# A decoder layer on one core: the part behind the experts, with the order of its products changed

## The chip, the cores and the metric

The kernel runs on one core of one Trainium2 chip. A core has TensorE (PE: matrix products, results in PSUM), VectorE (DVE), ScalarE (ACT), GpSimd (POOL) and SyncE (SP, which here only issues DMAs). Each engine works through its own list of instructions in order, and engines wait for one another by semaphores. PSUM has eight banks of 128 x 512 f32. The metric is the device time of one launch in microseconds (us); lower is better.

## The reference, cut to what matters

One layer for 1024 prompt positions and 8 x 4 sample positions. Up to the experts, nothing is changed. Behind them, what is computed is

```python
h = h + hierarchical_moe(...)                          # 16 experts, each token uses two
e = rms_norm(p_i @ w_ple, norm_ple)                    # (rows, 256) @ (256, 1024)
gate = jax.nn.sigmoid(rms_norm(h, norm_pg) @ w_pg)     # (rows, 1024) @ (1024, 1024)
h = h + gate * e
y = rms_norm(h, norm_final)
```

The rows are 1056, so there are nine tiles of up to 128 rows; the last one has 32.

## The kernel before

**Products.** A product in f32 is made from three products in a reduced format: each operand is split into a high part (rounded by ScalarE) and a low part (the rest, by VectorE), and `product3` (L711 to L719) issues for each 128 of the contraction high x high (L716), low weight x high (L717) and high weight x low (L718). A tile's embedding product (`c_ple`) is 12 matmuls of 512 columns, its gate product (`c_gate`, two halves) is 48. `transposes` (L463) turn 128 x 128 blocks through PSUM: 8 for a tile's normalised rows (`c_rows`), 2 for its embedding input (`c_embed`).

**Experts.** A block is 128 gathered rows through one expert. Weights of expert e+1 are split in pieces A0, A1, B, D0, D1 (ScalarE L1471, L1476; VectorE L1187, L1177) while expert e runs. After a block its result is copied to `yb` and stored to `y_rows` (L1521). For the part behind the experts, `w_pg` takes the place of an expert's gate and up weights (A0, A1, B) and `w_ple` that of its down weights (D0). In the last block, B and D0 are split only after the block's result has been copied out.

**The part behind the experts** works tile by tile on one set of buffers. Its first tiles and last tiles are written out, those between are loops (`Fori`).

- SP waits until the last block has been stored, then raises `blocks_over` (L433 to L435), and loads the embedding input of a tile (`p_load`, L424) and stores the output of the tile before (L429).
- POOL, `c_gather` (L1731 to L1740): the two expert results of each row are fetched by two indirect DMAs into `ya` and `y2`, after the indices have been copied to `index_u` (L1737). The gather of tile t+2 waits for `c_head` of tile t+1. POOL also computes the factors of the three norms (`rstd`: L1634, L1636, L1638) and the normalised rows `an` (L1747).
- DVE, `c_head` (L1262, L1264): h += gate weight x gathered row, twice. `c_en` (L1282, L1285) scales the embedding product, `c_blend` (L1293, L1295) forms h + gate x e, `c_out` (L1302) writes the output row; `c_anT` and `c_pT` make the low parts (L1177).
- ACT: sums of squares of h (`c_hsq`, L1565), of the embedding product (`c_esq`, L1570, L1571) and of the final h (`c_fsq`, L1581), the sigmoid (L1576), and the high parts (`c_pT` L1551, `c_anT` L1557, L1559).
- PE: for each tile gate half 0, embedding transposes of the next tile, gate half 1, row transposes of the next tile, embedding product of the next tile. ACT starts the stage with `c_hsq(0)`, and so does DVE with `c_head(0)`; the first embedding product waits behind both.

## Time and profile before

| | |
|---|---|
| runs (3) | 1328.31, 1332.95, 1333.29 us; median 1332.95 |
| profiled execution, its own time (span, first to last instruction) | 1329.0 us |
| mean granted clock of TensorE, of 2.4 GHz | 0.962 |
| busy: PE, DVE, ACT, POOL | 1211.2 (91%), 701.7 (53%), 505.0 (38%), 213.2 us (16%) |
| last matmul of the last block, first product of the stage | 1141.8 us, 1158.4 us |
| last product of the stage, end | 1318.3 us, 1329.0 us |

The trace is one execution. Times in the rows are from the start of the span. `1.00` as granted clock is 2.4 GHz, the lower level is 1.2 GHz. A bracket behind a row is the idle time of that engine before it and what ended it. Durations of matmuls overlap, so that the distance between two starts is the cost of one.

### The profile page before, as it was taken

The numbers are of one execution on the slowest core, as the hardware profiler recorded it, in microseconds if no ns is written. First come the engines' busy times: TensorE is split into PE (matmuls) and PEld (weight loads), VectorE is DVE, ScalarE is ACT, GpSimd is POOL, SyncE is SP. The second block draws the span as 40 slices with busy tenths as digits, with TensorE's granted clock in tenths as the row PEclk, the third lists the DMA queues.
The fourth block names the chain that finished last, engine by engine and source line by source line (L and its number), as shares of the span: only waits on it lengthen the run. The fifth ranks groups of instructions, "written<-read, shape, count | busy, mean of one in ns | idle before, by whom it ended". The sixth has DMA issues, their size and how long they took to land.

```text
span 1329.0 us, 17507 instructions
## 1 busy us (share of the span) xinstructions
PE 1211.2 (91%) x6065; PEld 860.7 (65%) x6066; DVE 701.7 (53%) x1343; ACT 505.0 (38%) x860; POOL 213.2 (16%) x336
## 2 busy tenths in 40 slices
PE   2999999999999999989659999999999999599886
PEld 1454555565655554435259899988989999477663
DVE  1344343434343434333665986599966662545454
ACT  0222222213131313121325875588855551433332
POOL 3320202020202020010100000000000000254452
PEclk9999999999999999998669999999999999799998
DMA  9700000000000000024394995599996564223320
GB/s 317 288 1 1 16 0 16 0 16 0 16 0 16 0 17 0 19 73 151 122 289 169 374 369 209 215 373 369 376 368 219 203 212 159 68 68 103 103 76 36
DMA packets 122092, 180.28 MB, mean 136 GB/s; under 512 B 7795, under 2 KB 96479, under 8 KB 122066
## 3 DMA queue, kind: packets, MB, share of 16 engines
q1 hardware_dynamic: 108078, 144.60, 31.9%
q0 software_dynamic: 6512, 21.77, 4.8%
q10 hardware_dynamic: 7476, 13.57, 2.7%
q8 instruction: 15, 0.25, 0.1%
q14 instruction: 11, 0.09, 0.0%
HBM read 151.96 MB, written 27.96 MB: 135 GB/s over the span
## 4 chain that ended last, share of the span: by engine, by line
PE 71%; DMA 7%; DVE 7%; ACT 5%; POOL 5%; issue 3%; ACTq 2%; SPq 0%; POOLq 0%; DVEq 0%
PE bank L457 36%; PE bank L716 10%; PE bank L718 9%; PE bank L717 9%; PE bank L463 4%; DMA raw_gu<-in_w_up 3%; DMA rows<-y_rows,index_u 3%; PE bank L629 1%; DVE w_lo L1187 1%; POOL work_c L1747 1%; POOL small L1636 1%; POOL small L1634 1%; ACT w_hi L1471 1%; DVE work L982 1%; ACT L1415 1%
## 5 line engine op out<-in xcount | busy, mean ns | idle before, releaser
L457 PE MATMUL bank<-weights,work 128*128 128x512 f32 (+3 forms) x1152 | 456.0, 553 | 1.9 <-DVE work L851 1.5
L457 PEld LDWEIGHTS bank<-weights,work 128*128 128x128 f32 (+1 forms) x1152 | 196.2, 182 | 242.4 <-issue 241.7
L716 PE MATMUL bank<-w_hi,xh 128*128 128x256 f32 x768 | 220.3, 287 | 2.7 <-DVE xl L1177 2.7
L718 PE MATMUL bank<-w_hi,xl 128*128 128x256 f32 x768 | 218.2, 284 | 0.0
L717 PE MATMUL bank<-w_lo,xh 128*128 128x256 f32 x768 | 218.2, 284 | 0.0
L1187 DVE SCALAR_TENSOR_TENSOR w_lo<-raw_gu,cols,w_hi 128x512 fp32r<-128x512 f32 x272 | 183.2, 746 | 8.9 <-ACT w_hi L1471 8.2
L1471 ACT ACTIVATE w_hi<-raw_gu,cols 128x512 fp32r<-128x512 f32 x272 | 170.5, 714 | 32.4 <-PE bank L718 19.0
L716 PEld LDWEIGHTS bank<-w_hi,xh 128*128 128x128 f32 x768 | 147.9, 193 | 4.2 <-issue 3.1
L717 PEld LDWEIGHTS bank<-w_lo,xh 128*128 128x128 f32 x768 | 148.1, 193 | 0.8
L718 PEld LDWEIGHTS bank<-w_hi,xl 128*128 128x128 f32 x768 | 147.9, 193 | 0.0
L1634 POOL TENSOR_TENSOR small<-small,norm_c 128x1 f32<-128x1 f32 (+1 forms) x54 | 24.2, 448 | 531.9 <-ACT work L1411 297.2
L716 PE MATMUL bank<-w_hi,hid_hi 128*128 128x512 f32 x192 | 78.5, 409 | 0.0
L1177 DVE TENSOR_TENSOR w_lo<-raw_d,w_hi 128x1024 fp32r<-128x1024 f32 x66 | 77.5, 1216 | 0.1
L885 DVE COPY work<-bank 128x512 f32<-128x512 f32 (+1 forms) x9 | 6.2, 690 | 132.8 <-PE bank L457 132.8
L717 PE MATMUL bank<-w_lo,hid_hi 128*128 128x512 f32 x192 | 75.0, 391 | 0.0
L718 PE MATMUL bank<-w_hi,hid_lo 128*128 128x512 f32 x192 | 75.0, 390 | 0.0
L1720 POOL COPY index_u<-token_u 128x1 uint32 (+1 forms) x25 | 4.9, 198 | 427.6 <-PE bank L463 405.8
L851 DVE TENSOR_TENSOR work<-bank,cols 128x512 f32<-128x512 f32 (+1 forms) x27 | 16.5, 640 | 99.1 <-PE bank L463 99.1
L1476 ACT ACTIVATE w_hi<-raw_d 128x1024 fp32r<-128x1024 f32 x66 | 66.0, 1050 | 7.0 <-DVE yb L1232 4.0
L716 PE MATMUL bank<-w_hi,a_hi 128*128 128x512 f32 (+1 forms) x144 | 58.3, 405 | 2.7 <-DVE a_lo L1177 2.7
L1386 ACT ACTIVATE work<-bank 128x512 f32<-128x512 f32 (+1 forms) x9 | 5.4, 596 | 142.4 <-PE bank L457 142.4
L717 PE MATMUL bank<-w_lo,a_hi 128*128 128x512 f32 (+1 forms) x144 | 56.8, 395 | 0.0
(285 smaller groups left out, 1660.6 us busy)
## 6 DMA issues: line engine op xcount, KB each, us to landing
raw_gu<-in_w_gate SPq DMA_DIRECT2D x32, 1024.0 KB, 7.5
raw_gu<-in_w_up SPq DMA_DIRECT2D x32, 1024.0 KB, 10.2
raw_d<-in_w_down SPq DMA_DIRECT2D x16, 2048.0 KB, 12.4
y_rows<-yb ACTq DMA_DIRECT2D x24, 512.0 KB, 6.3
weights<-in_w_in SPq DMA_DIRECT2D x3, 2048.0 KB, 15.6
weights<-in_w_in SPq DMA_DIRECT2D x1, 4096.0 KB, 21.7
weights<-in_w_out SPq DMA_DIRECT2D x1, 4096.0 KB, 25.4
m_rows<-work SPq DMA_DIRECT2D x8, 512.0 KB, 2.6
```

The source lines that it names most:

```text
L457: last = nc.tensor.matmul(out, lhs(k), rhs(k), start=(k == ks[0]), stop=(k == ks[-1]))
L463: last = nc.tensor.transpose(out[:, (c - lo) * P:(c - lo) * P + T], src[0:T, c * P:c * P + w], ident[0:T, 0:T])
L629: last = nc.tensor.matmul(bank[4][0:T, hh * HP:(hh + 1) * HP], dec[0:T, hh, 0:T], xdt[0:T, hh * HP:(hh + 1) * HP], start=True, stop=True)
L716: nc.tensor.matmul(out, lh(k), rh(k), start=(k == 0), stop=False)
L717: nc.tensor.matmul(out, lh(k), rl(k), start=False, stop=False)
L718: last = nc.tensor.matmul(out, ll(k), rh(k), start=False, stop=(k == (K or len(ks)) - 1))
L851: return V.tensor_tensor(dst[:, :, 0:T], src_bank.rearrange("p (c t) -> p c t", c=4)[:, :, 0:T], bc(cols[:, c0:c0 + 4], P, 4, T), ALU.mult)
L1177: return V.tensor_tensor(out, x, hi.bitcast(F32), ALU.subtract)
L1187: ins = V.scalar_tensor_tensor(out=gu_lo[:, k, :, cols_], in0=raw_gu[q // KC][:, k, :, :], scalar=gain(e, k), in1=gu_hi[:, k, :, cols_].bi ...
L1471: ins = A.activation(gu_hi[:, k, :, cols_], raw_gu[q // KC][:, k, :, :], ACT.Copy, scale=gain(e, k))
L1476: ins = A.activation(d_hi[:, ks, :], raw_d[:, ks, :], ACT.Copy)
L1634: own.did(G.tensor_tensor(var[0:T], sum_[0:T], norm_eps[count][0:T, :], ALU.add))
```

## The change

- The stage is in two phases. First all nine embedding products, then all gate products. Everything is unrolled.
- The embedding products use three pairs of PSUM banks in turn (0/1, 4/5, 6/7), the gate products two pairs (0/1, 4/5), and transposed embedding inputs and transposed rows have banks 2 and 3. PSUM is declared as one tensor, so that one instruction can read two banks: the square, the scaling and the low and high parts of a tile are one instruction each where there were two.
- `e` is kept for all nine tiles (`en[t]`), and the output row is written over it. `ya`, `y2`, `p_in`, `p_hi`, `p_lo`, `a_hi`, `a_lo` exist twice; each tile has its own norm factors. The sigmoid is written in place in PSUM.
- `w_ple` is split inside the last block, into a place of its own (`wp_hi`, `wp_lo`), before the block's result is copied out. The second half of `w_pg` (B) is split during the first embedding products (`pg_hi`, `pg_lo`).
- Gathers of tiles 0 to 3 and the heads of tiles 0 and 1 fall into the first phase. Indices go to the indirect DMA without a copy. `c_blend` works on halves.
- Ahead of the stage only semaphores are merged under fewer names; the order of what waits for what is the same.

```diff
+        en = [placed(f"en{t}", (B0 + 4 * GU + 4 * D * t) if t < DC else (B0 + 4 * (GU + DN) + 4 * GU + 4 * D * (t - DC)) if t < 2 * DC else C1, D)[:, :]
+              for t in range(TILES)]
...
+            for t in range(2, TILES):
+                sp.wait_ge(s("pTp_done"), t - 1)
+                p_load(t)
+            sp.wait_ge(s("w_split"), PG_SPLIT)
+            sp.dma_start(fin_row, i["norm_final"].partition_broadcast(P)).then_inc(s("fin_row_loaded"), 16)
+            for t in range(TILES):
+                out_store(t)
...
+            def c_ple(t):
+                T = rows(t)
+                pe.wait_ge(s("pT_ready"), t + 1)
+                if t == 2:
+                    pe.wait_ge(s("bank6_free"), total1)
+                    pe.wait_ge(s("bank7_free"), total1)
+                if t >= 3:
+                    pe.wait_ge(s("en_ready"), t - 2)
...
+            def c_gate(t, half):
+                T = rows(t)
+                pe.wait_ge(s("anT_ready"), t + 1)
+                if t < 2:
+                    pe.wait_ge(s("en_ready"), TILES - 2 + t)
+                else:
+                    pe.wait_ge(s("blend_done"), 2 * t - 3 + half)
...
+            pe.wait_ge(s("w_split"), PLE_SPLIT)
+            for t in range(TILES):
+                c_ple(t)
+                if t + 2 < TILES:
+                    c_embed(t + 2)
+                if t == TILES - 2:
+                    c_rows(0)
+            pe.wait_ge(s("w_split"), PG_SPLIT)
+            for t in range(TILES):
+                c_gate(t, 0)
+                if t + 1 < TILES:
+                    c_rows(t + 1)
+                c_gate(t, 1)
...
                     split(e + 1, "A1")
+                    for k in range(PC):
+                        dve.wait_ge(s("w_high"), PG_A + k + 1)
+                        lo(wp_lo[:, k, :], raw_d[:, k, :], wp_hi[:, k, :]).then_inc(s("w_split"), 1)
                 dve.wait_ge(s("down_done"), n)
...
+            def c_head(t):
+                T = rows(t)
+                dve.wait_ge(s(f"ya{t % 2}_loaded"), 16 * (t // 2 + 1))
+                own.did(V.scalar_tensor_tensor(out=hrow(t), in0=ya[t % 2][0:T, :], scalar=gates[0:T, 0, t:t + 1], in1=hrow(t), op0=ALU.mult, op1=ALU.add))
+                dve.wait_ge(s(f"y2{t % 2}_loaded"), 16 * (t // 2 + 1))
+                own.wait()
+                V.scalar_tensor_tensor(out=hrow(t), in0=y2[t % 2][0:T, :], scalar=gates[0:T, 1, t:t + 1], in1=hrow(t), op0=ALU.mult, op1=ALU.add
+                                       ).then_inc(s("hc_ready"), 1)
...
+            def c_en(t):
+                T = rows(t)
+                dve.wait_ge(s("re_ready"), t + 1)
+                V.scalar_tensor_tensor(out=en[t][0:T, :], in0=pair((0, 4, 6)[t % 3])[0:T, :], scalar=re_[t][0:T, :], in1=ple_row[0:T, :],
...
+            def c_blend(t, half):
+                T = rows(t)
+                part = slice(half * BANK, (half + 1) * BANK)
+                dve.wait_ge(s("sig_ready"), 2 * t + half + 1)
+                if half == 0:
+                    dve.wait_ge(s("en_ready"), t + 1)
+                V.tensor_tensor(en[t][0:T, part], bank[(0, 4)[t % 2] + half][0:T, :], en[t][0:T, part], ALU.mult).then_inc(s("blend_done"), 1)
+                dve.wait_ge(s("blend_done"), 2 * t + half + 1)
+                V.tensor_tensor(hhalf(t, half), hhalf(t, half), en[t][0:T, part], ALU.add).then_inc(s("hf_ready"), 1)
...
+            c_pT(0)
+            c_pT(1)
+            pg_lo(range(0, 2))
+            dve.wait_ge(s("ple_row_loaded"), 16)
+            for t in range(TILES):
+                c_en(t)
+                if t + 2 < TILES:
+                    c_pT(t + 2)
+                if t < 3:
+                    pg_lo(range(2 * t + 2, 2 * t + 4))
+                if t == 2:
+                    c_head(0)
+                if t == 5:
+                    c_head(1)
+            c_anT(0)
+            dve.wait_ge(s("fin_row_loaded"), 16)
+            for t in range(TILES):
+                if t:
+                    c_blend(t - 1, 1)
+                if t + 2 < TILES:
+                    c_head(t + 2)
+                if t:
+                    c_out(t - 1)
+                c_blend(t, 0)
+                if t + 1 < TILES:
+                    c_anT(t + 1)
+            c_blend(TILES - 1, 1)
+            c_out(TILES - 1)
...
                     split(e + 1, "A1")
+                    act.wait_ge(s("d_loaded"), 16 * (NE + 1))
+                    act.wait_ge(s("w_split"), PG_A)
+                    for k in range(PC):
+                        A.activation(wp_hi[:, k, :], raw_d[:, k, :], ACT.Copy).then_inc(s("w_high"), 1)
                 act.wait_ge(s("down_done"), n)
...
                 act.dma_start(y_rows[bass.ds(b * P, P), :], yb).then_inc(s("y_stored"), 16)
-                if not more:
-                    split(e + 1, "B")
-                    split(e + 1, "D0")
...
+            def pg_hi(ks):
+                for k in ks:
+                    if k == 0:
+                        act.wait_ge(s("gu1_loaded"), 32 * (NE + 1))
+                    A.activation(gu_hi[:, k, :, HE:], raw_gu[1][:, k, :, :], ACT.Copy, scale=gain(NE, k)).then_inc(s("w_high"), 1)
...
+            def c_esq(t):
+                T = rows(t)
+                act.wait_ge(s("ple_done"), t + 1)
+                if t == TILES - 1:
+                    act.wait_ge(s("w_split"), PG_SPLIT)
+                A.activation(en[t][0:T, :], pair((0, 4, 6)[t % 3])[0:T, :], ACT.Square, accum_out=sse[t][0:T, :]).then_inc(s("sse_ready"), 1)
...
+            for t in range(TILES):
+                c_esq(t)
+                if t + 2 < TILES:
+                    c_pT(t + 2)
+                if t < 3:
+                    pg_hi(range(2 * t + 2, 2 * t + 4))
+                if t == 4:
+                    c_hsq(0)
+                if t == 6:
+                    c_hsq(1)
+            c_anT(0)
+            for t in range(TILES):
+                if t:
+                    c_sig(t - 1, 1)
+                if t + 2 < TILES:
+                    c_hsq(t + 2)
+                if t:
+                    c_fsq(t - 1)
+                c_sig(t, 0)
+                if t + 1 < TILES:
+                    c_anT(t + 1)
+            c_sig(TILES - 1, 1)
+            c_fsq(TILES - 1)
...
+            def c_gather(t):
+                T = rows(t)
+                if t >= 2:
+                    pool.wait_ge(s("hc_ready"), t - 1)
+                for q, dst, name in ((0, ya, "ya"), (1, y2, "y2")):
+                    pool.indirect_dma_start(dst[t % 2][0:T, :], None, y_rows[0:BLOCKS * P, :],
+                                            bass.IndirectOffsetOnAxis(ap=slots_u[0:T, q, t:t + 1], axis=0)).then_inc(s(f"{name}{t % 2}_loaded"), 16)
...
+            c_gather(0)
+            c_re(0)
+            c_re(1)
+            c_gather(1)
+            for t in range(2, 5):
+                c_re(t)
+            c_an(0)
+            c_gather(2)
+            for t in range(5, TILES):
+                c_re(t)
+            c_gather(3)
+            c_an(1)
+            for t in range(TILES):
+                if t:
+                    c_rf(t - 1)
+                if t + 2 < TILES:
+                    c_an(t + 2)
+                if t + 4 < TILES:
+                    c_gather(t + 4)
+            c_rf(TILES - 1)
```

## Rows read from the trace of the kernel before

**Rows 1.** The page: TensorE's busy tenths in 40 slices of the span

```profile
PE   2999999999999999989659999999999999599886
```

**Rows 2.** Busy times by stretch; columns: us, PE, PEld, DVE, ACT, POOL, PEclk, DMA

```profile
1224.10:1242.70 18.60, 16.74 (x79) 13.41 (x78) 9.15 (x11) 6.12 (x13) 9.12 (x15) 1.00 0.26 92
```

**Rows 3.** Chain that ended last, at the stage's begin; columns: start, us, what

```profile
1142.86 2.62 DMA y_rows<-yb
...
1146.40 1.19 POOL rows L1739
...
1148.39 5.24 DMA rows<-y_rows,index_u
...
1156.42 1.15 ACT work_c L1565 x2
1157.57 0.28 ACT p_hi L1551
1157.87 0.44 DVE p_lo L1177
```

**Rows 4.** The same chain, through one tile of the loop

```profile
1205.42 1.16 ACT work_c L1565 x2
...
1209.01 1.90 POOL work_c L1747
...
1214.86 6.17 DMA rows<-y_rows,index_u
1221.29 1.30 DVE h L1262
...
1224.14 1.16 ACT work_c L1565 x2
```

**Rows 5.** TensorE in order of time, one tile; start, us, line, operation, count

```profile
1180.23 1.04 PE L463 MATMUL bank<-ident,work_c 128*128 128x128 f32 x8
1181.02 0.47 PE L716 MATMUL bank<-w_hi,p_hi 128*128 128x512 f32 x1
...
1183.90 0.50 PE L716 MATMUL bank<-w_hi,a_hi 128*128 128x512 f32 x1
...
1195.18 1.03 PE L463 MATMUL bank<-ident,work_c 128*128 128x128 f32 x8
```

**Rows 6.** TensorE in order of time, after idle times (in brackets)

```profile
1158.44 0.77 PE L716 MATMUL bank<-w_hi,p_hi 128*128 128x512 f32 x1 [16.42 <-DVE p_lo L1177]
...
1163.70 1.10 PE L463 MATMUL bank<-ident,work_c 128*128 128x128 f32 x8
...
1248.28 1.09 PE L463 MATMUL bank<-ident,work_c 128*128 128x128 f32 x8 [1.59 <-POOL work_c L1747]
1251.13 0.50 PE L716 MATMUL bank<-w_hi,p_hi 128*128 128x512 f32 x1 [1.76 <-DVE p_lo L1177]
...
1255.23 0.63 PE L716 MATMUL bank<-w_hi,a_hi 128*128 128x512 f32 x1
```

**Rows 7.** VectorE and ScalarE in order of time, around the experts' end

```profile
1138.64 2.73 DVE L1187 SCALAR_TENSOR_TENSOR w_lo<-raw_gu,cols,w_hi 128x512 fp32r<-128x512 f32 x4
...
1148.17 1.99 ACT L1476 ACTIVATE w_hi<-raw_d 128x1024 fp32r<-128x1024 f32 x2
...
1149.32 2.35 DVE L1177 TENSOR_TENSOR w_lo<-raw_d,w_hi 128x1024 fp32r<-128x1024 f32 x2
```

**Rows 8.** VectorE in order of time, in the first tile

```profile
1166.09 1.29 DVE L1177 TENSOR_TENSOR a_lo<-bank,a_hi 128x512 fp32r<-128x512 f32 x2 [7.80 <-ACT a_hi L1559]
...
1170.96 0.75 DVE L1282 SCALAR_TENSOR_TENSOR work_c<-bank,small,ple_row 128x512 f32<-128x512 f32 x1
```

**Rows 9.** The chain that ended last, its end

```profile
1318.35 0.59 ACT work_c L1576
...
1321.52 1.05 ACT work_c L1581
...
1323.90 1.27 DVE rows L1302
```

436 lines of the change are left out of this document (157 added, 279 removed).

## The prediction

> **What bounds the kernel now.** I read the page first, for where TensorE is less than full: it is busy in nine tenths of nearly every slice, and the dip near the end is where the changed stage begins [rows 1]. Everything ahead of the last block is untouched, so the question is the 187.2 us from the last block's last matmul (1141.8) to the end (1329.0). Second, the chain that ended last, at the stage's begin: result stored, indices copied, gathers issued, rows landed at 1153.6, the head of h, its square, and only then the first embedding input is split [rows 3], so that TensorE stands still for 16.42 us, although the embedding product needs nothing of h [rows 6]. Third, the same chain inside the loop: it runs through square, norm, gather, a transfer of 6.17 us and the head, from 1205.42 to 1224.14, 18.7 us for a tile [rows 4], and TensorE comes into it nowhere. TensorE's own work for a tile is 15.0 us (1180.23 to 1195.18, without idle time) [rows 5]; in a loop tile it is busy for 16.74 of 18.6 us [rows 2] and pays short waits, of which some pull its clock down. So the stage is bound by a chain through one pair of gather buffers, some 3.7 us a tile above TensorE.
>
> **Prices.** From starts in [rows 5], at 2.4 GHz: 8 row transposes 0.8, embedding product 2.9, two gate halves with 2 embedding transposes between 11.3 (a half 5.6). At 1.2 GHz an embedding product takes 5.26 (1158.44 to 1163.70) [rows 6]. A square of 1024 columns takes 1.2 [rows 4]; a square and the norm factor behind it 2.4 (1321.52 to 1323.90) [rows 9]; a low part of 1024 columns 1.3, of 256 columns 0.4 [rows 3, 8]; a head 2 x 1.3 [rows 4]; scaling by `c_en` is two halves of 0.75 now and one instruction afterwards, 1.3 to 1.5, I take 1.3 since a head instruction of that width takes that [rows 4, 8]; a pair of gathers is two issues of 1.2 [rows 3]. The sigmoid that writes PSUM has no row. Its nearest is the one that writes SBUF, 0.6 [rows 9]; I take 0.6 and give it 0.5 to 0.8.
>
> **Step 1, the start.** In the last block VectorE ends piece A1 at 1141.37 [rows 7]. Behind it now come two copies for `wp_hi` on ScalarE (1.0 each, to 1143.4) and two low parts on VectorE (1.18 each, to 1144.9) [rows 7]. Queued behind these are the copies of the result to `yb`: VectorE's half ends at 1145.6, so the store, issued at 1142.86 now, and `blocks_over` come 2.8 us later. Who waits for that is the gathers, and they no longer stand before TensorE. ScalarE, which issues the store, goes on at 1146.2; high and low part of the first embedding input (0.3 and 0.4 [rows 3]) give the first product at 1147.1 instead of 1158.4: **11.3 us gained**. TensorE idles 5 us there, not 16.4.
>
> **Step 2, nine embedding products.** TensorE would need 9 x 2.9 + 7 x 0.15 + 0.8 = 28 us. But it is not what bounds them. The input of tile t+2 is split by VectorE behind `c_en(t)`, hence: end of product t, square and norm 2.4, `c_en` 1.3, low part 0.4, and some 0.3 of signalling, 4.4 us until product t+2 may start. Two tiles then take 4.4 + 2.9 = 7.3 us, 3.7 a tile. Twice it is worse. `c_head(0)` (2.6) and pieces of `w_pg` (1.4) are queued on VectorE ahead of `c_en(3)`: product 5 is about 2 us late. On POOL the normalised rows of tile 0 (factor 1.2, rows 1.90 [rows 4]) and the gather of tile 2 (2.4) are queued ahead of the norm factor of tile 5: product 7 is some 1.2 us late. `c_head(1)` then holds VectorE ahead of `c_en(6)`, and with it the input of product 8, by about 1 us. Laid out instruction by instruction, with product 0 at 5.1 (low clock after 5 us idle), this gives the products' starts 1147.1, 1152.4, 1156.7, 1160.4, 1164.0, 1169.7, 1172.7, 1178.1, 1182.3 and the last end at 1185.2. Then a seam: the first gate product waits for square and norm of tile 8 (2.4), `c_en(8)` 1.3 and the low part of the rows of tile 0, 1.3, together 5.2 with signalling: 1190.4. I add 2 us for product starts at the low clock after the idle times of 2 to 3 us, part of it hidden, and 1 us for POOL, whose small operations are slower beside VectorE: **first gate product at 1193.5**.
>
> **Step 3, nine gate products.** TensorE: 18 x 5.57 + 8 x 0.8 = 106.7. The chain here, from the end of gate half 1 of a tile: sigmoid 0.6, blend of half 1 1.4, head of a later tile 2.7, its square 1.2, final square and norm 2.4, output row 1.3, blend of half 0 1.4, low part 1.3, signalling 0.4: 12.7 us until the gate product after next may start. TensorE is free for it after 11.95 (one tile). The rest, 0.75, is paid every second tile, or 0.4 a tile: 3.2 in all. One more low-clock piece behind the 5 us seam: in the loop before, 1.59 and 1.76 us of idle time close together were followed by an embedding product of 4.1 us (1251.13 to 1255.23) instead of 2.9 [rows 6]; I take 1.6. Last gate product ends at 1193.5 + 106.7 + 3.2 + 1.6 = **1305.0**, against 1318.3.
>
> Gathers stand on nothing here: the gather of tile t+4 is issued in tile t, and 6.2 us of transfer [rows 4] lie beside two tiles of 12. If that cover were gone, each tile would pay up to 6 us.
>
> **Step 4, the end.** 10.7 us from the last matmul to the end now. The blend works on the half that is left, two operations of 0.65 instead of two of 1.22: 1.1 less. End 1305.0 + 9.6 = 1314.6.
>
> **The sum.** 1329.0 - 1314.6 = 14.4 us in the profiled execution, whose span lies 4 us under the median of the runs. Taken from the median: 1332.95 - 14.4 = **1319**. Its own range is 1312 to 1326 (`c_en` and sigmoid at either end, signalling, clock). The seam of unrolled code has no price in the trace: the two unrolled last tiles of before show no idle time other than that for data, so I put it at 0 to 2 us.
>
> **Rivals.** (a) The clock stays at 2.4 GHz: a loop tile in which TensorE did nothing for 1.9 of 18.6 us has a granted clock of 1.00 [rows 2], and the new idle times are mostly 0.7 us a tile. Then the 2 and 1.6 fall away, and most of the slow first product is hidden anyway by the chain; POOL isn't slowed (1 us): -19.0, 1314. 18%.
> (b) The opposite: TensorE is at 80% in the embedding phase, with an idle time in every tile, and stays at 1.2 GHz there. Nine products of 5.26 with their transposes are 50 us, now themselves the bound, and the first gate product starts at 1203.8; the time is 1329, no change that can be told. For it: 1.59 + 1.76 us of idle time were enough once [rows 6]. 12%.
> The Trainium skill, "TensorE: Matmul & The Clock Gate", section "A second HAM failure mode: psum-queue depth-cycling", speaks for (b): products that cycle through PSUM banks with micro-idle times between them make the clock swing. By it the sum would be that of (b) or a little under; by the single rows above it is mine.
> (c) The chain of step 3 is longer, for instance because POOL's norm factor meets a busy VectorE (from the square's end at 1206.58 to 1209.01 it took 2.4 us in the loop [rows 4], against 1.2 at the end) and VectorE's order makes everybody wait. At 14.7 us instead of 12.7 each tile costs 1 us more, 7 to 8 us in all: 1326. 10%.
> (d) Slower than before: as (b), and the low clock lasts into the gate products, since now they wait in every second tile. A 512-column matmul costs 0.2 us more there [rows 6], so beyond (b) it takes 54 of them, little more than one tile, to be 0.5% slower; at two tiles 1348. Against it: gate tiles keep TensorE 97% busy. 6%.
> My forecast 54%.
>
> **Numbers.** 0.5% (6.7 us) is about what a measurement of this kernel can tell from no change; the runs of before spread by 5 us. Faster: forecast, (a) and half of (c), 77%; same: (b) and the rest of (c), 17%; slower: 6%. The range reaches from (a) with its own 4 us to (b): 1309 to 1330.
>
> **What would show it.** In the profile of the changed kernel: the first embedding product 5 us behind the last block's last matmul (step 1); starts of embedding products 3.5 to 4 us apart, with TensorE waiting for the low part of the embedding input (step 2); 5 us of idle time before the first gate product; gate tiles 12.3 us apart, with no wait for gathered rows anywhere (step 3); 9.6 us at the end (step 4). It is wrong if the granted clock is low through the first phase, if gate tiles are over 13 us apart, or if a gather or a load of embedding input ends a wait.

## The result and the profile after

| | before | after |
|---|---|---|
| median of the runs | 1331.01 us (4 runs, 1328.31 to 1333.29) | 1311.30 us (4 runs, 1310.36 to 1311.70) |
| ratio, 95% interval | | 0.9852 [0.9832, 0.9872] |
| profiled execution, span | 1329.0 | 1309.2 |
| mean granted clock | 0.962 | 0.967 |
| last block's end to first product | 16.8 | 5.6 |
| first product to end of the last | 159.9 | 153.5 |
| end of the last product to the end | 10.7 | 9.5 |

The change makes the kernel 1.5% faster, some 20 us where 14.4 were predicted. Of the 19.8 us between the two spans, 1.0 lies ahead of the stage, where the work is the same. The rest is 11.2 at the start, 6.4 between the products and 1.2 at the end.

Since the time ahead of the stage differed by up to 2.6 us from trace to trace with the same work in it, I compare below the *stage*: from TensorE's transposes of the first embedding inputs (right behind the last block's last matmul, at 1141.64 before and 1140.64 after) to the end. It is 187.4 us before and 168.6 after.

The page after, TensorE and its granted clock in 40 slices. It answers to [rows 1], where slice 35 is at 5 tenths and slices 38 and 39 at 8. Now slices 35 to 37, the embedding phase and the seam behind it, are at 7 to 8 tenths, 38 and 39 are full, and the clock's last dip lies in slice 37. The dips around slice 20 lie ahead of the stage in both.

```profile
PE   2999999999999999998749999999999999878997
...
PEclk9999999999999999997759999999999999998999
```

Busy times by stretch: the wait at the start, the embedding phase, the seam, the gate phase, the end. Columns as in [rows 2]: us, PE, PEld, DVE, ACT, POOL, granted clock, DMA share, GB/s.

```profile
1140.60:1146.20 5.60, 0.64 (x5) 0.37 (x4) 3.52 (x5) 3.32 (x6) 0.00 (x0) 0.74 0.11 45
1146.20:1185.20 39.00, 32.15 (x130) 23.90 (x130) 22.66 (x28) 17.43 (x35) 19.13 (x34) 0.91 0.38 123
1185.20:1190.10 4.90, 0.03 (x1) 0.02 (x1) 2.59 (x4) 2.01 (x3) 3.01 (x5) 0.75 0.11 13
1190.10:1299.70 109.60, 108.53 (x496) 84.56 (x496) 60.15 (x64) 34.90 (x56) 51.70 (x67) 0.98 0.26 89
1299.70:1309.20 9.50, 0.00 (x0) 0.00 (x0) 2.63 (x3) 1.71 (x3) 0.95 (x3) 0.71 0.06 14
```

TensorE is full in the gate phase (108.53 of 109.60) and in no other stretch. In the embedding phase it does nothing for 7 of 39 us. (The seam is the idle time between the last embedding product and the first gate product.)

TensorE after, in order of time; brackets as in [rows 6]. These are the transposes at the stage's begin, products 0, 2, 5 and 7 (counted from 0), the row transposes of tile 0, the first gate half, the row transposes behind it, and one of the later gate products that had to wait.

```profile
1140.64 0.60 PE L467 MATMUL psum<-ident,p_in 128*128 128x128 f32 x4
...
1146.22 0.77 PE L720 MATMUL psum<-wp_hi,p_hi 128*128 128x512 f32 x1 [4.98 <-DVE p_lo L1174]
...
1155.18 0.50 PE L720 MATMUL psum<-wp_hi,p_hi 128*128 128x512 f32 x1 [0.99 <-DVE p_lo L1174]
...
1168.31 0.50 PE L720 MATMUL psum<-wp_hi,p_hi 128*128 128x512 f32 x1 [2.17 <-DVE p_lo L1174]
...
1176.98 0.51 PE L720 MATMUL psum<-wp_hi,p_hi 128*128 128x512 f32 x1 [2.44 <-DVE p_lo L1174]
...
1181.43 1.04 PE L467 MATMUL psum<-ident,an 128*128 128x128 f32 x8
...
1190.11 0.76 PE L720 MATMUL psum<-w_hi,a_hi 128*128 128x512 f32 x1 [4.88 <-issue]
...
1197.68 1.03 PE L467 MATMUL psum<-ident,an 128*128 128x128 f32 x8
...
1216.33 0.50 PE L720 MATMUL psum<-w_hi,a_hi 128*128 128x512 f32 x1 [0.37 <-DVE a_lo L1174]
```

Every wait of the embedding phase ends with the low part of an embedding input (products 2, 3, 4, 5 and 7 wait, for 0.99, 0.48, 0.74, 2.17 and 2.44 us; 1, 6 and 8 do not). The first product stands behind 4.98 us of idle time instead of 16.42 [rows 6]. The first gate half takes 7.6 us (1190.11 to 1197.68) where one takes 5.6 at full clock [rows 5].

The chain that ended last, after, through one gate tile; start, us, what. It answers to [rows 4].

```profile
1204.21 0.59 ACT psum L1586
...
1204.83 0.70 DVE en L1292
...
1206.24 1.21 DVE h L1263
...
1208.86 1.16 ACT dump L1574 x2
...
1210.10 1.16 ACT dump L1594 x2
...
1211.60 0.58 POOL small L1646
...
1213.73 0.69 DVE en L1292
...
1214.44 0.69 DVE h L1294
...
1215.14 1.14 DVE a_lo L1174
...
1216.33 0.50 PE psum L720
```

The gathers have gone from the chain; the sigmoid, both halves of the blend, a head, two squares and the norm are what is left. From 1204.18, the end of a product, to 1216.33 this takes 12.15 us. TensorE's own work between these two points takes 11.78, and the rest, 0.37, is the idle time in the row of 1216.33 above. Such a wait occurs three times in the whole phase.

### The profile page after: what moved, and what is told of

Read it like the earlier page. It is cut to its first block, busy times and chain, and to the rows that moved or that the text cites. A ratio compares the mean times of both kernels' runs of the same rounds, so it can differ in the third digit from the quotient of the medians.

```text
span 1309.2 us, 17273 instructions
## 1 busy us (share of the span) xinstructions
PE 1208.6 (92%) x6065; PEld 859.7 (66%) x6066; DVE 702.2 (54%) x1343; ACT 501.1 (38%) x833; POOL 203.6 (16%) x309
## 4 chain that ended last, share of the span: by engine, by line
PE 75%; DVE 9%; ACT 4%; issue 4%; DMA 3%; POOL 2%; ACTq 2%; DVEq 0%; SPq 0%; POOLq 0%; another core or an unknown queue 0%
PE psum L461 36%; PE psum L720 11%; PE psum L722 10%; PE psum L721 10%; PE psum L467 5%; DVE w_lo L1184 2%; DMA raw_gu<-in_w_up 1%; PE psum L633 1%; DVE work L979 1%; ACT L1410 1%; ACTq L1344 1%; PE psum L639 1%; DMA weights<-in_state_ssm 1%; DMA xg<-m_rows,index_u 1%; PE psum L616 0%
## 5 line engine op out<-in xcount | busy, mean ns | idle before, releaser
L461 PE MATMUL psum<-weights,work 128*128 128x512 f32 (+3 forms) x1152 | 455.7, 552 | 1.9 <-DVE work L848 1.5
L461 PEld LDWEIGHTS psum<-weights,work 128*128 128x128 f32 (+1 forms) x1152 | 196.2, 182 | 242.1 <-issue 241.4
L720 PE MATMUL psum<-w_hi,xh 128*128 128x256 f32 x768 | 220.3, 287 | 2.7 <-DVE xl L1174 2.7
L722 PE MATMUL psum<-w_hi,xl 128*128 128x256 f32 x768 | 218.2, 284 | 0.0
L721 PE MATMUL psum<-w_lo,xh 128*128 128x256 f32 x768 | 218.2, 284 | 0.0
L720 PEld LDWEIGHTS psum<-w_hi,xh 128*128 128x128 f32 x768 | 147.8, 193 | 4.2 <-issue 3.1
L721 PEld LDWEIGHTS psum<-w_lo,xh 128*128 128x128 f32 x768 | 148.0, 193 | 0.8
L722 PEld LDWEIGHTS psum<-w_hi,xl 128*128 128x128 f32 x768 | 147.8, 192 | 0.0
L1644 POOL TENSOR_TENSOR small<-small,norm_c 128x1 f32<-128x1 f32 (+1 forms) x54 | 17.2, 319 | 553.3 <-ACT work L1406 297.2
L720 PE MATMUL psum<-w_hi,hid_hi 128*128 128x512 f32 x192 | 78.6, 409 | 0.1
L722 PE MATMUL psum<-w_hi,hid_lo 128*128 128x512 f32 x192 | 75.1, 391 | 0.0
## 6 DMA issues: line engine op xcount, KB each, us to landing
raw_d<-in_w_down SPq DMA_DIRECT2D x16, 2048.0 KB, 12.1
```

What stands on the lines that cost most here:

```text
L461: last = nc.tensor.matmul(out, lhs(k), rhs(k), start=(k == ks[0]), stop=(k == ks[-1]))
L720: nc.tensor.matmul(out, lh(k), rh(k), start=(k == 0), stop=False)
L721: nc.tensor.matmul(out, lh(k), rl(k), start=False, stop=False)
L722: last = nc.tensor.matmul(out, ll(k), rh(k), start=False, stop=(k == (K or len(ks)) - 1))
L1644: own.did(G.tensor_tensor(var[0:T], sum_[0:T], norm_eps[count][0:T, :], ALU.add))
```

## The experiments

Stage lengths and starts are from one trace each, ratios from the medians of 3 to 5 rounds. "Start" is from the stage's begin to the first embedding product, "middle" from there to the last product's end.

| kernel | stage | start | middle | ratio to before [95%] |
|---|---|---|---|---|
| before | 187.4 | 16.8 | 159.9 | |
| after | 168.6 | 5.6 | 153.5 | 0.9852 [0.9832, 0.9872] |
| e1_unroll | 182.8 | 16.6 | 155.4 | 0.9954 [0.9940, 0.9969] |
| e2_gather_first | 179.0 | 17.2 | 151.1 | 0.9941 [0.9924, 0.9958] |
| e9_old_order | 172.3 | 16.8 | 144.7 | 0.9901 [0.9886, 0.9917] |
| e3_head_first | 178.7 | 14.9 | 154.3 | 0.9929 [0.9912, 0.9946] |
| e4_one_set | 168.4 | 5.5 | 153.3 | 0.9859 [0.9842, 0.9875] |
| e5_split_late | 168.6 | 5.6 | 153.4 | 0.9869 [0.9852, 0.9886] |
| e12_kept_busy | 164.9 | 5.6 | 149.8 | 0.9840 [0.9827, 0.9853] |
| e6_pT_first | 166.1 | 5.6 | 151.0 | 0.9829 [0.9816, 0.9843] |
| e7_seam | 166.1 | 5.6 | 150.9 | 0.9846 [0.9833, 0.9860] |
| e8_both | 163.6 | 5.6 | 148.5 | 0.9816 [0.9803, 0.9830] |
| e10_tuned | 160.9 | 5.6 | 145.8 | 0.9822 [0.9809, 0.9835] |
| e11_tuned_early | 160.7 | 3.7 | 147.4 | 0.9823 [0.9804, 0.9843] |

### One part of the change alone, in the kernel before

**e1_unroll** writes out the five loops of the stage and leaves everything else.

```diff
-            with pe.Fori(1, NT - 1) as t:
-                c_tile(t, pe.snap(t + 1))
+            for t in range(1, NT - 1):
+                c_tile(t, t + 1)
```

> The kernel before with the five loops of the last stage written out and nothing else changed. In its loop, instructions that wait for a register's value show 0.15 to 0.4 us of idle time each (head to head, norm factor to rows, copy of the index to gather), some 1.0 to 1.3 us in the chain of one tile; six tiles are in the loops. My theory: 6 to 8 us faster, 0.995 of before. Rival (the gain is in the order and the buffers, unrolling gives nothing): 1.000. Rival (unrolling is most of it): 0.985.

The stage is 4.6 us shorter, less than the 6 to 8 expected. The chain that ended last, one tile of e1_unroll, start, us, what: squares of h in two tiles that follow one another.

```profile
1203.21 1.16 ACT work_c L1565 x2
...
1221.08 1.16 ACT work_c L1565 x2
```

A tile is 17.9 us instead of 18.7 [rows 4], through the same operations. Of the 0.85 us, some 0.55 are short idle times of the kind that the expectation names (norm factor to rows, index copy to gather, landed rows to head, head to head: 0.1 to 0.2 us less each), and 0.25 is the transfer behind the second gather, 5.92 us instead of 6.17. The prediction had spoken only of the seams of unrolled code, at 0 to 2 us; that loops cost something, it had not priced.

**e2_gather_first** keeps the loops and moves GpSimd's gather of tile t+2 ahead of the normalised rows and of the final norm factor.

```diff
                 c_re(t, n)
+                if not (isinstance(t, int) and t >= NT - 1):
+                    c_gather(t + 2, None, n2)
                 if rows(t) != S:
                     c_an(t + 1, n2)
                 if p is not None:
                     c_rf(t - 1, p)
-                if not (isinstance(t, int) and t >= NT - 1):
-                    c_gather(t + 2, None, n2)
```

> The kernel before, loops and single buffers kept; only on POOL the gather of tile t+2 is placed ahead of the normalised rows of tile t+1 and the final norm factor. Head 2.7, two index copies and issues 2.5 to 3, transfer 5 to 6, head: 11 to 12 us, shorter than TensorE's 15.0. My theory (the loop was bound by POOL's order, which put norm and rows into the gathers' chain): tiles come every 15 to 16 us instead of 18.7, 14 to 20 us faster, 0.987. Rival (one set of gather buffers is what binds): 18 us a tile still, 0.998 to 1.000.

The expectation was too high: the stage is 8.4 us shorter, a tile 16.9 us. Of e2_gather_first: GpSimd's normalised rows, VectorE's output row, and embedding products of two tiles in TensorE's list, each in order of time.

```profile
1208.27 1.89 POOL L1747 TENSOR_TENSOR work_c<-h,small 128x1024 f32<-128x1024 f32 x1 [0.19 <-POOL small L1638]
...
1211.39 1.28 DVE L1302 SCALAR_TENSOR_TENSOR rows<-h,small,rows 128x1024 f32<-128x1024 f32 x1 [6.09 <-POOL small L1638]
...
1213.06 0.50 PE L716 MATMUL bank<-w_hi,p_hi 128*128 128x512 f32 x1 [0.34 <-DVE p_lo L1177]
...
1229.95 0.53 PE L716 MATMUL bank<-w_hi,p_hi 128*128 128x512 f32 x1 [1.75 <-DVE p_lo L1177]
```

The gather has left the chain, as it should, and a second queue stands behind it. GpSimd computes the final norm factor only after the normalised rows (till 1210.16), VectorE stands idle for 6.09 us before its output row that needs the factor, and the low part of the next embedding input is queued on VectorE behind the output row. So TensorE waits for something that never needed the factor.

**e9_old_order** takes e1 and e2 together and also moves VectorE's output row behind the low parts.

```diff
                 c_en(t, n)
-                if p is not None:
-                    c_out(t - 1, p, ...)
                 if more:
...
                     c_anT(t + 1, n2)
+                if p is not None:
+                    c_out(t - 1, p, ...)
```

> The kernel before with one set of buffers, tile by tile as it was, in three orders only: loops written out; on POOL the gather of tile t+2 ahead of the normalised rows of tile t+1; on VectorE the low parts for tile t+1 ahead of the output row of tile t-1, which in the run with the gather first had become what TensorE waited for. Theory (the loop's loss was the order on the helping engines, not the tile-by-tile plan): tiles 15.0 to 15.8 us apart instead of 18.7, last product 18 to 22 us earlier, start of the stage as before: 14 to 19 us faster than before, 0.987. Rival (tile by tile can't be brought near TensorE's 15 us): over 16.5 us a tile, 0.992 or above.

The stage is 15.1 us shorter with one set of buffers, one tile at a time; between the medians it is 12.7 us, less than the 14 to 19 expected. TensorE in e9_old_order, row transposes of tiles that follow one another:

```profile
1210.29 1.09 PE L463 MATMUL bank<-ident,work_c 128*128 128x128 f32 x8 [0.89 <-POOL work_c L1747]
...
1226.33 1.10 PE L463 MATMUL bank<-ident,work_c 128*128 128x128 f32 x8 [0.86 <-POOL work_c L1747]
```

A tile is 16.04 us, of which TensorE's work is 15.0 [rows 5] and 0.86 is this wait. The middle is 144.7 us, **8.8 us shorter than that of the changed kernel**. So the two phases are not what makes the middle shorter: the order in the lists of GpSimd and VectorE does it, and the embedding phase, where TensorE idles, gives a part of that back. What the changed kernel has over e9_old_order is the start: 11.2 us, and for that it does need the phases. In e9_old_order GpSimd ends the normalised rows of tile 0, which need gathered rows, at 1161.92, and TensorE turns them at 1163.78, right behind the first embedding product. Had that product come earlier, the gate product behind it could have come at most 1.9 us earlier. The changed kernel fills that time with further embedding products.

### One part of the change undone

**e3_head_first** puts the head of tile 0 ahead of the first embedding input on VectorE, as it stood before.

```diff
+            c_head(0)
             c_pT(0)
...
-                if t == 2:
-                    c_head(0)
```

> The changed kernel with VectorE's head of tile 0 moved back ahead of the first embedding input, as before the change. Theory: the first embedding product starts 16 to 17 us behind the last block's last matmul instead of 5.6; product 5 no longer waits for that head (2 us back); the kernel is 8 to 10 us slower than the changed one, 0.992 of before. Rival (the early start is lost again in waits behind it, since the gathers and norms come no earlier): 0 to 2 us slower than the changed one, 0.986.

TensorE in e3_head_first, the first embedding product:

```profile
1156.03 0.77 PE L720 MATMUL psum<-wp_hi,p_hi 128*128 128x512 f32 x1 [14.27 <-DVE p_lo L1174]
```

The start is 14.9 us instead of the 16 to 17 expected, the stage 10.1 longer. Products 4 and 5 start 3.7 us apart, 5.4 in the changed kernel, where that head stands between them: the 1.7 us come back, as expected. A single place in VectorE's list carries most of what the start gained, since in it stands the wait for a store and two gathers.

**e4_one_set** uses one pair of gather buffers (`ya[0]`, `y2[0]`) for all tiles and puts the gather of tile t+3 first in GpSimd's tile.

```diff
-                if t >= 2:
-                    pool.wait_ge(s("hc_ready"), t - 1)
+                if t >= 1:
+                    pool.wait_ge(s("hc_ready"), t)
...
-                    pool.indirect_dma_start(dst[t % 2][0:T, :], ...
+                    pool.indirect_dma_start(dst[0][0:T, :], ...
...
             for t in range(TILES):
+                if t + 3 < TILES:
+                    c_gather(t + 3)
                 if t:
...
-                if t + 4 < TILES:
-                    c_gather(t + 4)
```

> The changed kernel with one set of ya and y2 instead of two: a gather waits for the head of the tile before, and stands on POOL right behind that head's turn. Theory (two sets aren't needed when POOL's order is right; head 2.7 + issue 2.4 + transfer 5 is 10 to 11 of 12 us): gate tiles stay 12.0 to 12.5 us apart, 0 to 2 us slower than the changed one, 0.985 to 0.987 of before. Rival (the second set is what took the gathers out of the chain): gate tiles 14 us or more apart, 10 us or more slower, 0.993 or above.

Stage and median stay as they were. GpSimd in e4_one_set, first gathers of two tiles:

```profile
1219.96 1.06 POOL L1747 DMA_INDIRECT ya<-y_rows,slots_u  x1 [3.88 <-DVE h L1266]
...
1232.53 1.06 POOL L1747 DMA_INDIRECT ya<-y_rows,slots_u  x1 [4.67 <-DVE h L1266]
```

GpSimd idles until a head has freed the buffers, for 3.9 to 4.7 us in the later tiles (2.78 and 7.15 at the first two), and the rows have a tile of 12 us to come. Only the head of tile 2, at the seam, waits for its rows (2.45 us), and TensorE does not wait for it. Once the gather stands first in GpSimd's tile, the second pair of gather buffers buys nothing. One pair with the gather in its old place wasn't tried in this plan.

**e5_split_late** splits `w_ple` behind the copies of the last block's result instead of ahead of them.

```diff
-                    for k in range(PC):
-                        dve.wait_ge(s("w_high"), PG_A + k + 1)
-                        lo(wp_lo[:, k, :], raw_d[:, k, :], wp_hi[:, k, :]).then_inc(s("w_split"), 1)
                 dve.wait_ge(s("down_done"), n)
...
                 V.tensor_copy(yb[:, BANK:], bank[7][:, :]).then_inc(s("bank7_free"), 1)
+                if not more:
+                    for k in range(PC):
+                        ...
```

> The changed kernel with the split of w_ple moved back behind the copy of the last block's result, on ScalarE and VectorE. Theory (the early start comes from the embedding products no longer standing behind the head, not from where w_ple is split): result stored 2 to 3 us earlier, w_ple split 2 to 3 us later but next to the same copies, first embedding product 5.5 to 6 us behind the last block's last matmul as in the changed kernel; 0 to 1 us, 0.985 of before. Rival (the split inside the block bought part of the start): the first product 2 to 3 us later, 0.987.

No change: 168.6 us, first product after 5.60 instead of 5.58, although the result's store is issued 2.9 us earlier, counted from the stage's begin. The four pieces have to be done before the first product on either side of the copies.

### What the low clock costs

**e12_kept_busy** adds 18 matmuls of 512 columns, whose results nobody uses, in each of the two 5 us stretches in which TensorE had nothing to do.

```diff
             pe.wait_ge(s("xT_ready"), total1)
+            for _ in range(18):
+                nc.tensor.matmul(bank[0][:, :], hid_hi[:, 0, :], ...
             pe.wait_ge(s("w_split"), PLE_SPLIT)
...
             pe.wait_ge(s("w_split"), PG_SPLIT)
+            pe.wait_ge(s("en_ready"), TILES - 2)
+            for _ in range(18):
+                nc.tensor.matmul(bank[0][:, :], wp_hi[:, 0, 0:P], ...
```

> The changed kernel with 18 matmuls of 512 columns that nothing uses in each of TensorE's two idle times of 5 us (before the first embedding and before the first gate product). It adds work and should only keep the clock up. Theory: first embedding product 2.9 instead of 4.8 us, first gate half 5.7 instead of 7.7, 3 to 4 us faster than the changed kernel, 0.982 to 0.983. Rival (what follows waits for other chains, so that the clock costs nothing at the first place): 2 us, 0.984. Rival (the clock falls all the same): 0 to 1 us slower, 0.986.

TensorE in e12_kept_busy, in order of time: the unused matmuls at the start, product 0, the first gate half behind the unused matmuls of the seam.

```profile
1141.11 4.35 PE L810 MATMUL psum<-hid_hi 128*128 128x512 f32 x18
...
1146.34 0.47 PE L720 MATMUL psum<-wp_hi,p_hi 128*128 128x512 f32 x1 [0.88 <-DVE p_lo L1179]
...
1188.44 0.50 PE L720 MATMUL psum<-w_hi,a_hi 128*128 128x512 f32 x1 [0.74 <-DVE a_lo L1179]
```

Busy times by stretch in e12_kept_busy, the embedding phase with the seam, and the gate phase; columns as above.

```profile
1146.30:1188.40 42.10, 34.82 (x148) 25.78 (x148) 25.27 (x31) 19.36 (x38) 23.12 (x39) 0.96 0.34 115
1188.40:1296.10 107.70, 106.64 (x496) 83.07 (x496) 60.25 (x64) 34.90 (x56) 51.81 (x67) 1.00 0.26 90
```

The chains are as they were (only the transposes of tile 2 now wait 0.33 us for their load), and TensorE starts each phase at full clock: product 0 takes 3.0 us instead of 4.8 (to the end of its last matmul), and the granted clock of the gate phase is 1.00 instead of 0.98. From the stage's begin the first gate product comes after 47.7 us instead of 49.5, and the last one ends after 155.4 instead of 159.0. So work in these two idle times gives back 1.8 us ahead of the gate phase and 1.9 in it, 3.7 in all. That is not the whole cost of the low clock: product 7, behind 0.87 us, is now at full clock, but product 5, behind 2.20 us, fell to the low one (4.38 us from its start to the transposes behind it), which it did not behind 2.17 us in the changed kernel (2.86). The medians' interval does not tell this kernel from the changed one; the trace does.

### Better orders within the new plan

**e6_pT_first** puts the split of the embedding input of tile t+2 ahead of the square and the scaling of tile t, on both engines (ScalarE has the same exchange with `c_esq`).

```diff
             for t in range(TILES):
-                c_en(t)
                 if t + 2 < TILES:
                     c_pT(t + 2)
+                c_en(t)
```

> The changed kernel; in the embedding phase ScalarE and VectorE split the embedding input of tile t+2 ahead of the square and the scaling of tile t instead of behind them. Theory (these products wait for a chain through square, norm and scaling that they don't need): products 3.0 to 3.3 us apart, first product to the end of the ninth 30 to 34 us instead of 39, 5 to 8 us faster than the changed kernel, 0.980 of before. Rival (VectorE or the norms are the limit anyway, since the third pair of banks comes free only behind the scaling): starts stay 3.6 us or more apart, 0.985.

TensorE in e6_pT_first, product 5:

```profile
1167.74 0.50 PE L720 MATMUL psum<-wp_hi,p_hi 128*128 128x512 f32 x1 [3.29 <-DVE p_lo L1174]
```

The theory holds up to product 4: products 2 to 4 start 3.0 to 3.4 us apart from the one before instead of 3.7 to 4.2. Then product 5 waits 3.29 us, because its input is now queued directly behind the head of tile 0, and it runs at the low clock. What was expected to fall to 30 to 34 us, first product to end of the ninth, is 36.7. The stage is 2.5 us shorter where 5 to 8 were expected.

**e7_seam** splits the normalised rows of tile 0 before the square and the scaling of tile 8.

```diff
             for t in range(TILES):
+                if t == TILES - 1:
+                    c_anT(0)
                 c_en(t)
...
-            c_anT(0)
```

> The changed kernel; the rows of tile 0 are split ahead of the square and scaling of tile 8. Theory: the 4.9 us of idle time between the last embedding product and the first gate product go down to 1 us or less, and with them the piece at 1.2 GHz behind it (first gate half 5.7 instead of 7.7 us): 5 to 6 us faster than the changed kernel, 0.981 of before. Rival (the clock falls there whatever the idle time): 3 to 4 us, 0.983.

TensorE in e7_seam, the first gate half and the row transposes behind it:

```profile
1187.59 0.47 PE L720 MATMUL psum<-w_hi,a_hi 128*128 128x512 f32 x1 [0.44 <-issue]
...
1196.43 1.09 PE L467 MATMUL psum<-ident,an 128*128 128x128 f32 x8 [3.12 <-POOL an L1759]
```

The seam has closed, from 4.88 us to 0.44, and the first gate half runs at full clock (5.7 us). But then TensorE waits 3.12 us for the normalised rows of tile 1, which GpSimd computes behind the norm factor of tile 8 and the gather of tile 3. That gives half of it back: the stage is 2.5 us shorter where 5 to 6 were expected.

**e8_both** has both edits.

> Both orders of the two kernels above together. Theory: the gains add, 10 to 13 us faster than the changed kernel, 0.976 of before. Rival (the first is only a shift of waits to the seam or the heads): no more than the better of the two alone, 0.980 to 0.981.

163.6 us, 5.0 shorter: the sum of the two, not the more that was expected, though for another reason than I thought. Product 5 still waits for 3.29 us. The wait of 3.12 us for the rows of tile 1 has gone, but in its place the seam is 1.86 us and the first gate half takes 7.3 us again, at the low clock.

**e10_tuned** takes e8 and moves the waits' causes: the heads of tiles 0 and 1 are split in two, one instruction each in tiles 2 and 3, 5 and 6; the square of h of tile 1 comes a tile later; GpSimd computes the normalised rows of tile 1 ahead of the norm factor of tile 8.

```diff
-                if t == 2:
-                    c_head(0)
-                if t == 5:
-                    c_head(1)
+                if t in (2, 3):
+                    c_head(0, t - 2)
+                if t in (5, 6):
+                    c_head(1, t - 5)
...
             for t in range(5, TILES):
+                if t == TILES - 1:
+                    c_an(1)
                 c_re(t)
             c_gather(3)
-            c_an(1)
```

> The kernel with both orders (0.9816), and: the normalised rows of tile 1 on POOL ahead of the norm factor of tile 8 and the gather of tile 3 behind it; the heads of tiles 0 and 1 in two instructions in two different embedding tiles instead of one; the square of the head of tile 1 one tile later. Theory (in that kernel a head stands ahead of the split of an input, 3.3 us of idle time and a product at 1.2 GHz behind it, and the seam waits for the heads too): 3 to 5 us faster than it, 0.978 to 0.979. Rival (VectorE, busy for 26 of about 30 us in the embedding phase, is the limit): 0 to 1.5 us, 0.981.

The trace's stage is 2.7 us shorter than that of e8_both where 3 to 5 were expected, and the medians' intervals cover one another. In this trace the first gate half is at full clock behind a seam of 1.86 us, as long as that of e8_both, which makes 1.8 of the 2.7 us; that the new order gave them isn't shown. Product 5 still waits 1.94 us and TensorE now waits 2.40 us before the row transposes of tile 0, until VectorE has read the last embedding input from the bank that they write.

**e11_tuned_early** takes e10 and splits the first two embedding inputs in the last block, ahead of the copies of its result.

```diff
+                    for k in range(2):
+                        dve.wait_ge(s("ph_ready"), k + 1)
+                        lo(p_lo[k][:, :, :], bank[2 + k]...).then_inc(s("pT_ready"), 1)
                 dve.wait_ge(s("down_done"), n)
...
-            c_pT(0)
-            c_pT(1)
```

> The one above, and the first two embedding inputs are split inside the last block, ahead of the copies of its result. Theory: first embedding product 3.6 to 3.9 us behind the last block's last matmul instead of 5.6; gathers 0.8 us later, which nobody waits for; 1.5 to 2.5 us faster than the one above. Rival (the later gathers come back as a wait of head 0): no gain.

TensorE in e11_tuned_early, behind product 0:

```profile
1150.67 0.44 PE L467 MATMUL psum<-ident,p_in 128*128 128x128 f32 x2 [1.36 <-DMA p_in<-in_p_prompt]
```

The first product comes after 3.7 us as expected, but the stage is only 0.2 us shorter instead of 1.5 to 2.5. The transposes of tile 2 now wait for its load, which SyncE issues behind its wait for the stored result, and with them product 1, which starts 9.85 us after the stage's begin instead of 10.08. Together e8, e10 and e11 are the fastest kernels here, at 0.982 of before, and the runs do not order them.

## Why the prediction was right, and where it was off

The time fell by more than predicted but within the range, 1311.3 against 1319 in 1309 to 1330. Of the 7.3 us between my unrounded sum (1318.55) and the median, 1.9 are the distance of a profiled span from its median, 4.0 before and 2.1 after. (Against the median of the four runs in the table, 1331.01, it is 2.0 before: the 4.0 came from a median of three runs and is nothing of the kernel.) 1.0 is the time ahead of the stage. The rest, 4.4, is in the terms of the sum.

**Step 1, the start: held.** 5.58 us from the stage's begin to the first product, 5.5 predicted. e3_head_first shows the cause by putting it back. One detail of it was idle: whether `w_ple` is split before or after the copies makes no difference (e5_split_late).

**Step 2, the embedding products: the layout held, the additions did not.** Starts from the stage's begin, in us:

| product | 0 | 1 | 2 | 3 | 4 | 5 | 6 | 7 | 8 | end |
|---|---|---|---|---|---|---|---|---|---|---|
| predicted | 5.5 | 10.8 | 15.1 | 18.8 | 22.4 | 28.1 | 31.1 | 36.5 | 40.7 | 43.6 |
| measured | 5.6 | 10.3 | 14.5 | 18.3 | 22.2 | 27.7 | 30.7 | 36.3 | 41.6 | 44.6 |

Both causes of late products are in the trace. VectorE after, in order of time: the head of tile 0 (its first instruction), `c_en(3)`, the low part for product 5, and `c_en(5)`.

```profile
1164.07 1.28 DVE L1263 SCALAR_TENSOR_TENSOR h<-ya,gates,h 128x1024 f32<-128x1024 f32 x1
...
1166.65 1.28 DVE L1278 SCALAR_TENSOR_TENSOR en<-psum,small,ple_row 128x1024 f32<-128x1024 f32 x1
1167.85 0.41 DVE L1174 TENSOR_TENSOR p_lo<-psum,p_hi 128x256 fp32r<-128x256 f32 x1
...
1175.31 1.28 DVE L1278 SCALAR_TENSOR_TENSOR en<-psum,small,ple_row 128x1024 f32<-128x1024 f32 x1 [5.36 <-POOL small L1648]
```

GpSimd after, in order of time: normalised rows of tile 0, the gather of tile 2 (its first issue), the norm factor of tile 5 (its first operation).

```profile
1169.70 1.90 POOL L1757 TENSOR_TENSOR an<-h,small 128x1024 f32<-128x1024 f32 x1
1171.76 1.07 POOL L1747 DMA_INDIRECT ya<-y_rows,slots_u  x1 [0.17 <-issue]
...
1174.10 0.21 POOL L1644 TENSOR_TENSOR small<-small,norm_c 128x1 f32<-128x1 f32 x1
```

`c_en(3)` starts only when the head ends, and product 5 behind it at 1168.31; the norm factor that `c_en(5)` needs (5.36 us of idle time before it) starts only behind the gather, and product 7 follows at 1176.98. The scaling over two banks (`c_en`), for which there had been no row, took 1.28 where I took 1.3.

I had then added 2 us for low clock and 1 for a slower GpSimd. The layout, with its seam of 5.2 us (4.88 measured), put the first gate product at 48.8 us; the additions made that 51.9 (0.1 of it a slip: 1190.4 and 3 are 1193.4, not 1193.5), and it came at 49.5. The addition was worth 0.7, not 3. Only product 7 ran at the low clock beyond product 0 (4.45 us to the transposes behind it instead of 2.9), and it held up product 8, whose input was there at 1180.83 and which started at 1182.22, behind it and the row transposes. GpSimd's slower factors cost nothing against the layout: that of tile 3 (2.3 us from its first operation to the end of its last) was covered by the head, that of tile 1 (2.0) made `c_en(1)` wait 0.79 us, and product 3 was still on time. **This term, 2.4 us, is over half of the error.** How little of it came true is in part luck: in the traces of e7_seam and e12_kept_busy product 5 fell to the low clock as well, behind the same idle time.

**Step 3, the gate products: right kind, smaller size.** 109.6 us from the first gate product to the end of the last, 111.5 predicted. TensorE's waits for the low part of rows are 1.0 us in all (three of 0.37 or less), not 3.2: the chain takes 12.15 us, not 12.7, and TensorE 11.8, not 11.95. A difference of two such numbers is small against the error of each, so 0.75 us every second tile was as good as unknown; it was 0.37, and only three times. The low clock behind the seam cost 2.0 (first half 7.6 instead of 5.6), against 1.6, and e12_kept_busy gives 1.9 back.

**Step 4, the end: held**, 9.5 against 9.6. **Gathers on nothing: held**, no engine waits for gathered rows in the gate phase.

**The rivals.** (b) is false: the granted clock of the embedding phase is 0.91, and of nine products only 0 and 7 ran at the low level, though four of the others (2 to 5) stand behind idle times of 0.5 to 2.2 us. The Trainium skill ("TensorE: Matmul & The Clock Gate", section "A second HAM failure mode: psum-queue depth-cycling"), weighed in the prediction, says that the clock swings when products cycle through PSUM banks with micro-idle times between them. The trace agrees in that the clock fell and rose again within the phase; it does not bear out what the prediction made of it, a whole phase at 1.2 GHz. (d) hangs on (b) and falls with it. (c): the chain was 12.1 us, not 14.7. (a) did not occur, the clock was low in three places, but e12_kept_busy is nearly that case: 3.7 us less, where (a) was 4.6 below the forecast.

**What the prediction missed** was less a number than a comparison. It explained the gain in the middle by the gathers taken off the chain, which is true, and read the loop as bound by "a chain through one pair of gather buffers". That second half is wrong: e9_old_order, with one pair and without phases, has the shorter middle, and e4_one_set, with one pair, loses nothing. I had read in [rows 4] that the gather is in the chain; I had not asked which instruction ahead of it in GpSimd's list put it there (normalised rows and a final factor, 1.9 + 1 us each tile). The two gains can't simply be added, though: the 11.2 us of the start need embedding products of many tiles to fill the time until the first gathered rows are there, which the tile-by-tile order does not have. With only its first embedding product moved, e9_old_order could gain 1.9 us at most, so that 172.3 - 1.9 = 170.4 us is an estimate for its stage, more than the 168.6 of the changed kernel. It wasn't tried.

## What to carry to other kernels

When a chain runs through engines that are half idle, look at what stands ahead of its links in those engines' lists before adding buffers: moving one gather ahead of the normalised rows and a final factor was worth 8.4 us, a second set of buffers nothing. After each such move read the next wait, since here every one that was removed (e2, e6, e7, e11) left another behind it, worth up to half of the gain or all of it. Of a stage with a long wait at its head, first move out of the queue what does not need what is waited for.

## What the runs showed of the hardware

- **The clock after idle time.** The traces of all kernels here, lengths from the start of a product to what follows it: behind 3.29 us of idle time and more, the product or gate half behind it ran at the low clock each time (behind some 5 us a product of 2.9 us took 4.4 to 5.3, a gate half of 5.6 took 7.4 to 7.9), unless unused matmuls filled the time. Behind idle times of 1.4 us and less it never fell in this stage. Between 1.7 and 3.1 us it went either way at the same length: product 5 was at full clock behind 2.17 us in the changed kernel (2.86 us) and low behind 2.15 in e7_seam (4.44), the first gate half low behind 1.86 us in e8_both and full behind 1.86 in e10_tuned. The same in the kernel before: a product took 4.10 us behind idle times of 1.59 and 1.76 [rows 6] and 2.85 behind 1.72 and 1.76 (from 1288.49). What decides there, these runs do not show; a single trace can be 1.2 to 2.4 us off a twin by it. Product 5 in e7_seam, the first gate half in e8_both and in e10_tuned; columns as in [rows 2]:

```profile
1170.40:1174.84 4.44, 4.44 (x13) 3.44 (x14) 1.62 (x2) 0.09 (x1) 3.86 (x6) 0.62 0.25 90
...
1185.98:1193.41 7.43, 7.33 (x25) 5.55 (x25) 3.75 (x3) 2.50 (x4) 6.59 (x9) 0.77 0.48 140
...
1185.14:1190.70 5.56, 5.56 (x24) 4.54 (x25) 3.40 (x3) 0.00 (x0) 4.70 (x6) 1.00 0.25 71
```

- **GpSimd beside VectorE.** The second of the three 128x1 operations of a norm factor (L1646) took 0.57 us in most rows, and up to 1.5 in some. GpSimd after, in order of time, the normalised rows of tile 2 and such an operation:

```profile
1198.87 1.90 POOL L1757 TENSOR_TENSOR an<-h,small 128x1024 f32<-128x1024 f32 x1 [3.10 <-PE psum L467]
...
1212.72 1.51 POOL L1646 TENSOR_TENSOR small<-small,half_neg 128x1 f32<-128x1 f32 x1
```

  VectorE after, an addition and the output row that run beside them:

```profile
1199.22 2.09 DVE L1294 TENSOR_TENSOR h<-h,en 128x512 f32<-128x512 f32 x1
...
1212.52 1.28 DVE L1299 SCALAR_TENSOR_TENSOR en<-h,small,fin_row 128x1024 f32<-128x1024 f32 x1 [3.70 <-POOL small L1648]
```

  The factor's operation started 0.2 us into VectorE's output row, which reads two operands from SBUF, with 1.08 us of it left, and took 0.94 longer than elsewhere. It also goes the other way: the addition, also with two operands in SBUF, started with 1.55 us of GpSimd's normalised rows left and took 1.40 us longer than its usual 0.69. A third case, normalised rows that started at 1214.63 with 0.50 us of an addition left, took 2.26 us instead of 1.90. The Trainium skill, "SBUF — State Buffer", section "SBUF: two separate sides", says that such an instruction of VectorE and one of GpSimd that reads SBUF exclude one another for the whole length of the one that started first. The three cases agree with it up to the same 0.15 us: the one that comes second is longer by nearly what was left of the first. No run here was made to test it.
- **Written-out loops.** 4.6 us for at most six turns of a loop on each engine, with the engines' operations in the chain at the same length. Beyond the one tile told at e1_unroll it was not taken apart.
- **PSUM.** The sigmoid in place took 0.57 to 0.59 us, as to SBUF (0.59, [rows 9]), and one scaling of 1024 columns over two banks 1.28, less than two of 0.75 [rows 8].
